# Block 1's loads and masks in another order, squares from PSUM at the norms, gate tiles moved between stages

## The reference, cut to what matters

```
x = x + 0.5 * rmsnorm(swiglu(rmsnorm(x, ffn1_pre_g), ...), ffn1_post_g)   # 1024 -> 2 x 2816 -> 1024
h = rmsnorm(x, mix_pre_g) @ w_qkv                                         # q, k, v of 16 heads
o = neighbourhood attention (8 heads, bias table + column mask),
    dilated mixture attention (8 heads, bucketed bias + window mask)
x = x + rmsnorm(concat(rmsnorm(o_na), rmsnorm(o_dil)) @ w_out, mix_post_g)
x = x + 0.5 * rmsnorm(swiglu(rmsnorm(x, ffn2_pre_g), ...), ffn2_post_g)

for l in (0, 1):                               # ctx: 256 more tokens, full in layer 0, state only in layer 1
    mx, mc = silu(c) @ w_mod + b_mod, silu(c_ctx) @ w_mod + b_mod         # six vectors of 1024 each
    h = rmsnorm(x) * g * (1 + scale) + shift
    forget gates, gated linear recurrence (4 heads, both directions), windowed attention with rope,
    2-D Fourier mix, 3072 sigmoid gates over three branches, w_out
    x = x + mx[2] * y;  x = x + mx[5] * relu(h2 @ w_ff1)**2 @ w_ff2
```

## Time and profile before

| | us |
|---|---|
| median of 3 runs | 2169.92 (2167.6 to 2171.84) |
| profiled execution | 2171.41 |
| its span | 2169.6 |
| PE busy | 2025.4 (93%) |
| DVE busy | 1277.9 (59%) |
| ACT busy | 949.1 (44%) |
| POOL busy | 490.6 (23%) |

### The profile page before, as it was taken

One profiled execution on the slowest core, in us unless ns is written; L12 is line 12 of the kernel. 1 busy time (PEld: TensorE's weight loads), 2 busy tenths in 40 slices (PEclk: granted clock), 3 DMA queues, 4 the chain that ended last, 5 costly groups with the idle time before them and its releaser, 6 DMA issues.

```text
span 2169.6 us, 30444 instructions
## 1 busy us (share of the span) xinstructions
PE 2025.4 (93%) x12228; PEld 1769.0 (82%) x12228; DVE 1277.9 (59%) x1993; ACT 949.1 (44%) x1525; POOL 490.6 (23%) x293
## 2 busy tenths in 40 slices
PE   7699798799989999979999899999989899988999
PEld 6699786699978888768578688888877898688999
DVE  5577797578865782533676475244356947775410
ACT  5344335455436333412564343133246354655643
POOL 0210010000000000000014555455510000056887
PEclk9899899899989999989999999999999999999999
DMA  7877381266732212211003244456523233134554
GB/s 259 236 282 259 112 274 63 87 209 229 252 136 88 69 49 78 88 52 65 20 30 107 97 136 153 138 186 202 193 98 107 83 130 112 56 113 141 185 186 155
DMA packets 84636, 299.23 MB, mean 138 GB/s; under 512 B 9992, under 2 KB 13200, under 8 KB 84112
## 3 DMA queue, kind: packets, MB, share of 16 engines
q1 hardware_dynamic: 64512, 231.76, 30.9%
q0 software_dynamic: 17280, 60.95, 8.9%
q10 hardware_dynamic: 2704, 4.57, 0.6%
HBM read 296.18 MB, written 4.11 MB: 138 GB/s over the span
## 4 chain that ended last, share of the span: by engine, by line
PE 77%; DVE 12%; ACT 4%; issue 3%; DMA 2%; POOL 2%; ACTq 0%; DVEq 0%; POOLq 0%
PE ps L457 21%; PE ps L452 21%; PE ps L455 21%; DVE wl L435 2%; ACT wh L419 1%; PE ps L1016 1%; PE ps L536 1%; DVE K L1656 1%; PE ps L1056 1%; PE ps L1033 1%; PE ps L959 1%; PE ps L961 1%; PE ps L964 1%; DMA naskew<-narel 1%; POOL wl L435 1%
## 5 line engine op out<-in xcount | busy, mean ns | idle before, releaser
L452 PE MATMUL ps<-HH,wh 128*128 128x256 f32 (+1 forms) x2336 | 771.2, 330 | 40.1 <-ACT HH L1284 10.7
L457 PE MATMUL ps<-HH,wl 128*128 128x256 f32 (+1 forms) x2336 | 757.1, 324 | 26.0 <-DVE wl L435 24.9
L455 PE MATMUL ps<-HL,wh 128*128 128x256 f32 (+1 forms) x2336 | 757.1, 324 | 1.4 <-DVE HL L1300 1.4
L435 POOL TENSOR_TENSOR wl<-wr,wh 128x1024 fp32r<-128x1024 f32 x166 | 413.0, 2497 | 969.6 <-ACT wh L419 964.9
L419 ACT ACTIVATE wh<-wr 128x1024 fp32r<-128x1024 f32 x440 | 460.2, 1052 | 326.3 <-PE ps L457 289.3
L452 PEld LDWEIGHTS ps<-HH,wh 128*128 128x128 f32 x2336 | 453.2, 194 | 85.9 <-issue 28.1
L457 PEld LDWEIGHTS ps<-HH,wl 128*128 128x128 f32 x2336 | 452.9, 194 | 61.5 <-DVE wl L435 26.9
L455 PEld LDWEIGHTS ps<-HL,wh 128*128 128x128 f32 x2336 | 453.2, 194 | 38.2 <-DVE HL L1300 3.0
L435 DVE TENSOR_TENSOR wl<-wr,wh 128x1024 fp32r<-128x1024 f32 x274 | 333.2, 1224 | 235.8 <-ACT wh L419 234.1
L2157 DVE SCALAR_TENSOR_TENSOR X<-ps,MOD,X 128x256 f32<-128x256 f32 x64 | 28.8, 480 | 246.9 <-PE ps L457 246.9
L457 PE MATMUL ps<-HIDH,wl 128*128 128x512 f32 (+1 forms) x512 | 173.1, 338 | 0.0
(11 more groups left out here) (253 smaller groups left out, 2649.2 us busy)
## 6 DMA issues: line engine op xcount, KB each, us to landing
wr<-wstream SPq DMA_DIRECT2D x440, 512.0 KB, 3.3
WM<-wmod POOLq DMA_DIRECT2D x68, 512.0 KB, 3.8
X<-wmod POOLq DMA_DIRECT2D x28, 512.0 KB, 5.4
NAB<-naskew POOLq DMA_DIRECT2D x16, 128.0 KB, 8.0
dilskew<-lines POOLq DMA_DIRECT2D x1, 2048.0 KB, 22.2
DILB<-dilskew POOLq DMA_DIRECT2D x2, 1024.0 KB, 11.9
COND<-cond ACTq DMA_DIRECT2D x2, 1024.0 KB, 4.6
CT<-consts POOLq DMA_DIRECT2D x1, 1216.0 KB, 9.5
```

Of the source, the lines that this page charges most:

```text
L435: ins = e.tensor_tensor(self.WL[i % NSPL][:, :], self.WR[n % NRAW][:, :], self.WH[i % NSPL][:, :].bitcast(F32), ALU.subtract)
L452: e.matmul(out, wh, xh, start=i == 0, stop=False)
L455: e.matmul(out, wh, xl, start=False, stop=False)
L457: ins = e.matmul(out, wl, xh, start=False, stop=i == n_k - 1)
```

## The change

- `pool_bias_loads`: modulation chunks 2 and 3 are loaded before POOL waits for the skewed table, 4 and 5 before it waits for the line, 6 and 7 behind the wide write.
- The masks become a generator. Two of the four are added in the first FFN at tiles 15 and 16, where no modulation step is taken (nor at tile 10), two in the down product's pairs ahead of modulation steps, of which there are up to five a pair instead of four; `dve_rows` takes a step in its first turn too.
- Pairs with squares: ACT squares the pair from PSUM, DVE waits for that and multiplies PSUM by the gain into Y. The sum of squares leaves its last tile to PE (`pe_root`). `dve_resid` works on four pairs instead of eight tiles.
- Norms without such sums square x in four pairs instead of eight tiles; PE still does eight matmuls.
- Layers' `dve_add_out` adds the square of the tile before ahead of the wait for the product; the eighth is left to PE.
- REC_FILLS, OUT_FILLS and `Fill.some` are changed: in layer 0 seven levels take 14 halves instead of 11, and rounds 4 to 9 one half instead of two; in layer 1 the levels take 19 instead of 17.

```diff
-REC_FILLS, OUT_FILLS = ((2, 1, 2, 1, 2, 1, 2), (2, 3, 2, 3, 2, 3, 2)), ((1, 1, 1), (2, 2, 1))
+REC_FILLS, OUT_FILLS = ((2, 2, 2, 2, 2, 2, 2), (3, 3, 3, 2, 3, 2, 3)), ((1, 1, 1), (1, 1, 1))
...
+    def act_pair_squares(self, e, w, key, ready):
+
+        self.act_squares(e, w, key, range(4), 512, lambda j: self.X[:, 2 * j:2 * j + 2, 0:256], ready)
...
     def pe_root(self, e, w, key, i, T, parts):
...
-        w.wait_ge(*self.c("sq_sum").at((key, i)))
+        w.wait_ge(*self.c("sq_sum").at((key, i - 1)))
         for p in range(parts):
-            ins = e.matmul(b[:, 0:T], self.ones, r[:, T * p:T * p + T], start=p == 0, stop=p == parts - 1)
+            e.matmul(b[:, 0:T], self.ones, r[:, T * p:T * p + T], start=p == 0, stop=False)
+        w.wait_ge(*self.c("sq").at((key, i)))
+        for p in range(parts):
+            ins = e.matmul(b[:, 0:T], self.ones, last[:, T * p:T * p + T], start=False, stop=p == parts - 1)
...
     def pe_norm(self, e, w, key):
-        self.pe_sum(e, w, key, 8, 256)
+        self.pe_sum(e, w, key, 4, 256, 2)
...
     act_pairs:
-                self.act_square(e, w, key, j, dst(j).rearrange("p h t -> p (h t)"), [self.c("out_cp").at((key, j))])
+                self.act_square(e, w, key, j, self.main.item((key, j))[:, :], [self.c("dense").at((key, j, 1))])
...
     dve_pairs:
                 for i, step in enumerate(self.steps((key, j, h), ks)):
                     self.make_low(e, w, "lo_dve", step)
-                    if i < 2 and (j, h) != (3, 1):
-                        next(mod, None)
+                    if i < 3 - h and (j, h) != (3, 1):
+                        next(side, None)
...
+            if gain:
+                self.dve_square(e, w, key, j - 1, 512)
             w.wait_ge(*self.c("dense").at((key, j, 1)))
-            ins = e.tensor_copy(dst(j), self.main.item((key, j))[:, :].rearrange("p (h t) -> p h t", h=2))
+            src = self.main.item((key, j))[:, :].rearrange("p (h t) -> p h t", h=2)
+            if gain:
+                w.wait_ge(*self.c("sq").at((key, j)))
+                ins = e.tensor_tensor(dst(j), src, bc(self.vec(gain, 2 * j, 2), 2, 256), ALU.mult)
+            else:
+                ins = e.tensor_copy(dst(j), src)
...
     dve_resid:
+        for j in range(4):
+            y, x = self.Y[:, 2 * j:2 * j + 2, :], self.X[:, 2 * j:2 * j + 2, 0:256]
+            w.wait_ge(*self.c("out_cp").at((key, j)))
+            e.tensor_tensor(y, y, bc(r, 1, 2), ALU.mult).then_inc(*self.c("resid").mark((key, j)))
+            w.wait_ge(*self.c("resid").at((key, j)))
+            ins = e.scalar_tensor_tensor(out=x, in0=y, scalar=half, in1=x, op0=ALU.mult, op1=ALU.add)
...
     pool_bias_loads:
+        for ch in range(2, 4):
+            self.pool_mod(e, w, 0, 0, ch)
         w.wait_ge(L["naskew"], 16)
...
-        self.pool_mod(e, w, 0, 0, 2)
-        self.pool_mod(e, w, 0, 0, 3)
+        for ch in range(4, 6):
+            self.pool_mod(e, w, 0, 0, ch)
         w.wait_ge(*self.c("skew").at("line"))
...
-        self.pool_mod(e, w, 0, 0, 4)
...
-        for ch in range(5, 8):
+        for ch in range(6, 8):
...
     dve_rows:
-            if k:
-                next(mod, None)
+            next(mod, None)
...
     dve_adaln:
-        if squares:
-            self.dve_square(e, w, squares, 7, 256 * len(cs))
...
     dve:
+        masks = self.dve_bias_masks(e, w)
+        for f in self.dve_ffn(e, w, 1, [], itertools.chain(masks, mod)):
             if f == 7:
                 self.dve_bias_line(e, w)
-            if f >= 2:
+            if f in (15, 16):
+                next(masks)
+            elif f >= 2 and f != 10:
                 next(mod)
...
         self.dve_norm(e, w, "n2", "mix_pre_g", self.low_of_group(e, w, "qk"))
-        self.dve_bias_masks(e, w)
...
-    def some(self):
+    def some(self, turn):
...
-        for _ in range(min(2 if self.last == 16 else 1, 44 - self.n)):
+        for _ in range(min(2 if self.last == 16 and not 4 <= turn < 10 else 1, 44 - self.n)):
```

More of the change, by code:

```diff
@@ L1 @@
+import itertools
 from contextlib import ExitStack
@@ L535, in pe_sum_add @@
         w.wait_ge(*self.c("n_sq").at((key, i)))
-        ins = e.matmul(self.aux.item((key, "sum"))[:, 0:T], self.ones, self.tm.item((key, "sq", i))[:, 0:T], start=i == 0,
-                       stop=i == n - 1)
+        for p in range(parts):
+            ins = e.matmul(self.aux.item((key, "sum"))[:, 0:T], self.ones,
+                           self.tm.item((key, "sq", i))[:, T * p:T * p + T], start=(i, p) == (0, 0),
+                           stop=(i, p) == (n - 1, parts - 1))
         ins.then_inc(*self.c("n_mm").mark((key, i)))
@@ L548, in act_squares @@
                 w.wait_ge(*x)
-            ins = e.activation(self.tm.item((key, "sq", i))[:, 0:T], src(i), ACT.Square)
+            out, ap = self.tm.item((key, "sq", i))[:, 0:T], src(i)
+            if len(ap.shape) == 3:
+                out = out.rearrange("p (h t) -> p h t", h=2)
+            ins = e.activation(out, ap, ACT.Square)
             ins.then_inc(*self.c("n_sq").mark((key, i)))
@@ L589, in pe_root @@
         self.aux.take((key, "sum"))
-        b, r = self.aux.item((key, "sum")), self.rm.item((key, "sq", 0))
+        b, r, last = self.aux.item((key, "sum")), self.rm.item((key, "sq", 0)), self.tm.item((key, "sq", i))
         for x in self.aux.before((key, "sum")):
             w.wait_ge(*x)
-        w.wait_ge(*self.c("sq_sum").at((key, i)))
+        w.wait_ge(*self.c("sq_sum").at((key, i - 1)))
         for p in range(parts):
-            ins = e.matmul(b[:, 0:T], self.ones, r[:, T * p:T * p + T], start=p == 0, stop=p == parts - 1)
+            e.matmul(b[:, 0:T], self.ones, r[:, T * p:T * p + T], start=p == 0, stop=False)
+        w.wait_ge(*self.c("sq").at((key, i)))
+        for p in range(parts):
+            ins = e.matmul(b[:, 0:T], self.ones, last[:, T * p:T * p + T], start=False, stop=p == parts - 1)
         ins.then_inc(*self.c("n_mm").mark((key, "root")))
+        self.tm.release((key, "sq", i), self.c("n_mm"), (key, "root"))
     def h_rhs(self, key, T=256):
@@ L662, in pe_pairs, with act_pairs @@
                 self.pe_squares(key, j)
-    def act_pairs(self, e, w, key, ks, pairs, dst, squares):
+    def act_pairs(self, e, w, key, ks, pairs, squares):
         if squares:
@@ L670, in act_pairs, with dve_pairs @@
             if squares:
-                self.act_square(e, w, key, j, dst(j).rearrange("p h t -> p (h t)"), [self.c("out_cp").at((key, j))])
-    def dve_pairs(self, e, w, key, ks, pairs, dst, squares, free, mod=iter(())):
+                self.act_square(e, w, key, j, self.main.item((key, j))[:, :], [self.c("dense").at((key, j, 1))])
+    def dve_pairs(self, e, w, key, ks, pairs, dst, gain, free, side=iter(())):
         for j in range(pairs):
@@ L749, in act_ffn, with dve_ffn @@
             yield f
-        self.act_pairs(e, w, ("down", n), range(22), 4, lambda j: self.Y[:, 2 * j:2 * j + 2, :], True)
-    def dve_ffn(self, e, w, n, y_free, mod):
+        self.act_pairs(e, w, ("down", n), range(22), 4, True)
+    def dve_ffn(self, e, w, n, y_free, side):
         for f in range(22):
@@ L766, in dve_ffn @@
             yield f
-        self.dve_pairs(e, w, ("down", n), range(22), 4, lambda j: self.Y[:, 2 * j:2 * j + 2, :], True, y_free, mod)
+        self.dve_pairs(e, w, ("down", n), range(22), 4, lambda j: self.Y[:, 2 * j:2 * j + 2, :],
+                       f"ffn{n}_post_g", y_free, side)
     def mod_steps(self, l):
@@ L1268, in act_adaln @@
         else:
-            for some in ([(k,) for k in range(8)] if spread else [range(8)]):
-                self.act_squares(e, w, key, some, c1 - c0, lambda k: self.X[:, k, c0:c1], ready)
-                if spread:
-                    yield
+            if not spread:
+                self.act_pair_squares(e, w, key, ready)
+            for k in range(8 if spread else 0):
+                self.act_squares(e, w, key, (k,), c1 - c0, lambda k: self.X[:, k, c0:c1], ready)
+                yield
             for x in self.rm.before(key):
                 w.wait_ge(*x)
-            self.act_root(e, w, key, c1 - c0, 1024, (key, 7), self.rm.item(key)[:, 0:c1 - c0])
+            self.act_root(e, w, key, c1 - c0, 1024, (key, 7 if spread else 3), self.rm.item(key)[:, 0:c1 - c0])
         yield
@@ L2153, in dve_add_out @@
             k = key + (d,)
+            if squares:
+                self.dve_square(e, w, key, d - 1, T)
             w.wait_ge(*self.c("dense").at(k))
@@ L2354, in act_layer @@
         if l == 0:
-            for _ in self.act_adaln(e, w, "norm 0 x", 0, 0, [0], lambda k: [self.c("x_new").at((("down", 2), k))],
+            for _ in self.act_adaln(e, w, "norm 0 x", 0, 0, [0], lambda j: [self.c("x_new").at((("down", 2), j))],
                                     [self.c("dense").at(("fu", 2, 21))],
@@ L2429, in dve @@
         context = self.dve_adaln(e, w, "norm 0 c", 0, 0, [1], spread=True)
```

(5 more changed lines are left out.)

58 lines of the change are left out of this document (23 added, 35 removed).

## The result

The changed kernel took **2102.6 us** (median of 4 runs, 2102.0 to 2112.9), the kernel before 2170.9 (median of 4). The ratio is **0.9699**, with a 95% interval of 0.9678 to 0.9721: 68 us won, where 61 were forecast. The profiled execution of the change is the slowest of the four, 2112.9 us; a second trace of the same kernel, on another chip, took 2102.8.

A forecast was written before the change was run, and what follows sets the result against it. PE (TensorE) was taken as the bound, busy 2025 of 2169.6 us, leaving idle time and lost clock to win. 15.5 + 10 + 9.3 + 3 + 17 + 4 + 2.5 = 61.3 us off 2171.4 gives 2110.1; range 2094 to 2138.

The forecast's parts named there:

- Part 1: Block 1's first FFN: earlier chunk loads end DVE's wait and PE's standstill; 15.5 us won, bounds 5 and 19.6.
- I take 4 us of new stall: First FFN: bias loads now compete with weights; 4 us of new stall come off the gain of at most 19.6.
- less 5 of lead: First FFN: weight blocks come 9 us late over the bias loads; the lows' lead of two blocks hides 5.
- The 10.6 us: First FFN: gain if weights get half while bias loads are queued and the lead is used up; sum then 2115.
- The rival of starved weights: First FFN: bias loads hold up weights, so ACT waits for its blocks; gain only 5 us, total 2121; chance 0.17.
- Part 2: q and k: masks moved ahead of the second norm let the first unit's scores come earlier; 10 us, bounds 6.5 and 12.5.
- Part 3: Norms between stages: shorter path through squares, root and residual; 9.3 us in block 1, 3 us at the layers' borders.
- Part 4: Gate halves moved from layer 0's rounds 4 to 9 into the recurrence: 17 us rounds, 4 layer 0's recurrence, 2.5 layer 1.
- the cap of 19.5 us: Layer 0's head rounds: three undisturbed rounds would take 37.3 of 56.8 us, so 19.5 is the most to win.
- The 2.5 us left for the heads' own chain: Layer 0's head rounds: allowance for ACT's and DVE's chain of Ln, Exp and four scalings, leaving 17 us won.
- the rival of rounds bound by their own chain: Layer 0's rounds: ACT and DVE no earlier, PE waits as long; 17 becomes 5, total 2122; chance 0.15.
- Layer 1's 2.5: Layer 1's recurrence: two more halves, and half clock behind its longest wait may go; 2.5 us, bounds -1 and 4.

The follow-up runs named there:

- the kernel with the norms alone: The kernel before with only the norms' change (squares from PSUM, residual in four pairs, last tile left to PE): 2158.5 us against 2168.0 beside it, ratio 0.9954.
- spread loads: The change with the 16 bias loads issued one per tile, tiles 7 to 14, and chunks 6 and 7 ahead of the 2 MB write: 2095.9 us, ratio 0.9659.

## Why the prediction was right, and where it was off

The forecast was 2110.1 us; 2102.6 came out, inside the range, and every part won. By its steps:

**Part 1, loads: mechanism right, size too high.** 15.5 us were forecast. The first trace has 12.3, the second 11.0 (13.0 less 2.0 of the norm), and undoing the order costs 11.5. The step that failed is "I take 4 us of new stall": it was 7.5. The rate was guessed well (4.6 us a block, 4.3 measured), and so were the queueing (bias loads against weights) and the 9 us of lateness: from 65.66 to 91.73 us ACT gets through six blocks, 26.1 us where PE needs 17.3, so they are 8.8 late. What was wrong is the "less 5 of lead": only 1.3 of the 8.8 were hidden. Part 1 itself had said that a wait of up to about 3 us is hidden, and two blocks of 2.9 us, less the 1.06 and 1.23 us in which ACT and DVE make the halves, leave 3.5 at the most (an estimate from these rows). The 8.4 us of the earlier trace rows, from 60 to 64 us, were no evidence for what lands beside all 16 bias loads. By the Trainium skill's rule (DMA: Bandwidth & Descriptors, section Queues, rings and completion order) that each DMA engine takes its queues in turn, the weights get half. The trace agrees: from 64 to 90 us the packets of the weights' queue took 53.1% of the engines' time and those of POOL's 50.6%. The 10.6 us that the forecast put beside that rule came nearer than my own term, but not by the rule, since my term had weights at half as well: they took the lead as used up. The rival of starved weights happened in part: ACT did wait for wr from 65 to 95 us, as the forecast named for its failure, but it cost 3.5 us more than assumed, not the 10.5 of the rival.

**Part 2, masks: right.** 10 us; the run without it gives 11.0 for q, k and v, and the first scores stand 72.1 us behind q's first product (71.5 forecast). What it left out is that part 1 needs it: without the three tiles that take no step, the new order of loads would lose 6.3 us to a late chunk 6.

**Part 3, norms: right,** 12.3 forecast, 12.0 found alone; 4.0 at w_out for 3.9, 2.5 for 2.7 at each FFN, 0.7, 0.7 and 1.6 for 0.75, 0.75 and 1.5.

**Part 4, gate halves: mechanism right in layer 0, too small.** 23.5 forecast, 30.5 found by the traces. In the rounds the failing term is the cap of 19.5 us, taken from the 56.8 us of three rounds. The fourth wait (0.77 us) and 10.2 us of half clock from 1054 us on lie outside that stretch, and both went with the rounds. The small waits behind the rounds did not help: 3.0 us before, 3.6 in the change. The kernel before, at 1054 us (columns as in the earlier trace rows):

```profile
1054.00:1064.20 10.20, 9.38 (x29) 5.48 (x29) 7.65 (x21) 6.65 (x17) 0.00 (x0) 0.52 0.01 2
```

The 2.5 us left for the heads' own chain was not needed: the rival of rounds bound by their own chain had no trace, PE waits for neither Q nor K. In the recurrence of layer 0 4 us were forecast under a bound of 5.7, and 6.0 came back: the waits went whole, and with them a little more. Layer 1's 2.5 came out as 1.9 to 2.6, but not by its mechanism: PE's waits there are hardly shorter (5.6 us before, 5.4 in the second trace), and 0.8 of the 2.6 lies ahead of the recurrence. That the number fits is luck.

Of the 32.7 us that layer 0 won between the two traces, 27.9 are part 4 and 0.7 its border. The other 4 are probably clock: the profiled execution of before had 133 us at half clock in all, the kernel with the norms alone 109, and that one wins 4.4 us in layer 0 with its 0.7 us of edit there.

The errors partly cancelled: 3 to 4.5 us too much in part 1, 7 too little in part 4, and some 4 us of clock that no part had. So part of the nearness of the sum is luck.

## What to carry to other kernels

When a stall is removed, ask what else then shares the stretch. Here the bias loads cost nothing while PE stood still, and 7.5 us when it ran; pacing them by PE's progress, with chunks 6 and 7 moved, won 8 us, beside the 11 to 12 of the new order of loads. POOL issues its loads in program order, so look for the next large transfer ahead of each small urgent one: both times the second loss sat behind the 2 MB write. Count a lead only as far as it is free: the time to make the halves comes off it. Take the cap of a gain from where the stage's last effect ends, half clock behind it included, not from the stretch in which the waits are seen.

## What the hardware showed that was not expected

- The row length of the loads did not matter here: 2 MB asked for at once slowed the weights' landing from 5.2 (spread loads) to 13.6 us in rows of 256 B and to 14.3 in contiguous rows of 8 KB, in packets of 2.7 and 4.1 KB on average.
- The clock stayed at half for 20.5 us with PE busy 20.46 of them, in narrow products (64 or 128 rows and 128 or 256 columns) behind a wait, in some executions and not in others: a wait of 4.66 and 4.65 us stands ahead of it in the two traces of the change, and half clock lasted 20.5 and 6.8 us. In the one trace with the wait filled by products of that kind it lasted 20.5 us too.
- Two executions of one kernel can so differ by 8 us in one stage. Without a second trace of the change, the units would have been read as slower by 4.5 us.
